# Decode rows laid out by head and token in the retention and state-space stages, and the last gate projection spread over the state-space tiles

## The chip, the cores and the metric

One core of a Trainium2 chip runs the whole program once per execution. The metric is device microseconds of that execution; the number compared is the median of several executions. Everything is float32.

## What is computed

A two-layer decoder trunk makes one inference step for two groups of rows with the same weights: a prompt of 512 tokens, and a sample group of 8 sequences with 4 tokens each (32 rows), which carries recurrent states from memory. Each layer projects the normalised input once (`w_in`), runs four mixers side by side, gates and merges their projections, projects back, and ends in a feed-forward block. Two mixers matter here. In both, every sample sequence `b` and head `h` has a 128x128 state that is read, used for the output, and written back:

```python
# retention, 4 heads; state-space (Mamba-2) has the same shape with B, C, x in place of k, q, v
intra = einsum('bhnm,bmhe->bnhe', scores, v)
cross = einsum('bnhd,bhde->bnhe', q * q_decay, S)
S_new = exp(log_gamma * C) * S + einsum('bmhd,bmhe->bhde', k * k_decay, v)
o = (o - mean(o)) * rsqrt(var(o) + eps) * silu(g)            # retention: per head
...
merged = sum_b sigmoid(gate_b) * (branch_b @ w_branch_b)     # gates: columns of h @ w_in
```

## The kernel before

All 544 rows (512 + 32) stay on chip. A layer is a chain of stages, each a block of five instruction streams (TensorE, VectorE, ScalarE, GpSimd, SyncE) written out by hand and tied by semaphores; all engines meet at a barrier between stages. The order is attention, retention (`stage_retention`), HGRN (`stage_hgrn`), state-space (`stage_ssm`: a convolution block, then the scan block), merge (`stage_merge`), feed-forward.

The mixers alone would leave TensorE idle, so the weight projections are dealt out among them. `jobs` lists the projections in order; the end of it is ..., gate20, wb11, gate21, wb20, gate30, wb21, gate31, wb30, wb31, wo0, wo1. A gate job is 64 matmuls (8 result rows of 8), a wb job 32 (8 rows of 4), each 128x128 by 128x272. The trace counts every float32 matmul as two records, so 16 records are 8 matmuls. A result row gets a PSUM bank from the set in `spare`; it must wait until the row that had the bank before has been taken out, by ScalarE for gates (with one sigmoid at the end of a job) and by VectorE for wb rows (a multiplication with the gate, L492, and an addition, L494). `Share(last, weights)` takes all matmuls up to the job `last` and cuts them at fixed points: where an engine's stream calls `share.point`, TensorE issues the matmuls up to that share, and ScalarE and VectorE take out rows that are done, one row behind. `stream` on SyncE loads the weights, each job into the slot of the job two before it, once that is finished.

Retention (L1285 to L1500) and the scan block of the state space (from L2087) run over five tiles: four of 128 prompt tokens, the fifth the 32 sample rows. The names used below:

- Retention, fifth tile. TensorE: scores L1327; fill; `A` times `v` L1335 and masked queries times states L1339 (8 per head, all writing rows 0 to 31 of bank 3), head by head, each waiting for a fresh mask `qm` from VectorE (L1431); then the added states `kd` times the spread values `Vx` L1355, eight matmuls that each wait for VectorE's update two before (L1442, a multiply-add; L1435 spreads `v` anew for every head); two points of fill; turning the result (L1361); fill. VectorE then normalises 32 rows of 512 (L1459 to L1469). SyncE stores the states (L1499).
- State space. Each tile: segment sums L2153; two points of fill; weights ready; outputs L2161, L2165, L2166 and the next tile's turns L2133 to L2137; two points of fill; wait for the finished rows `d_y`; turn them L2204; one point of fill. The fifth tile also turns the eight states and multiplies them (L2177, L2186), sums the decays (L2191, taken by ScalarE L2243), and updates the states: eight matmuls L2198, VectorE spreading `B` (L2305), decaying (L2308) and adding (L2309). The output chain on VectorE starts at L2318 and only after all updates. SyncE stores the sample states L2123, then the prompt state L2125.
- HGRN's fifth tile (L1638 on) has the layout that the change brings to the other two: rows by (head, token) on 128 partitions, so the four heads' matmuls use different strips of the array: L1683 for states, L1695 for updates, GpSimd decaying the states (L1563), VectorE adding (L1930), SyncE loading strips (L1953).
- `stage_merge` begins with gate31, then wb30.

Of the kernel before, what the change touches and what calls it, by code (L numbers as in the profile page):

```python
# [13 lines left out]
P = 128  # L14
# [28 lines left out]
for _n, _w in (("ident", 128), ("ones", 128), ("after", 128), ("tri", 128), ("lv_sum", 7 * 128), ("tri_s", 32), ("after_s", 32),  # L43
               ("seqhot", 8), ("qmask", 256), ("lv_mask", 6 * 32), ("lns", 1), ("rdec", 4 * 128), ("rq", 4), ("rk", 4), ("rdec_s", 4 * 32), ("rq_s", 4),
               ("rk_s", 4), ("cos", 5 * 64), ("sin", 5 * 64), ("neg", 128), ("neg_s", 32), ("eps", 1),
               ("rep", 2 * 128), ("wsel", 2 * NS), ("hsel", 8), ("sum4", NS), ("block", 1)):
    C[_n] = (_at, _w)
    _at += _w
# [4 lines left out]
def constants():  # L53
# [67 lines left out]
    put("block", r[:, None] % 32)  # L121
    put("hsel", (r[:, None] // TS) % 8 == np.arange(8)[None])
# [10 lines left out]
def trunk(nc, inp, out):  # L133

    es = ExitStack()
    with es:
# [187 lines left out]
        for name in ("gate30", "wb21"):  # L324
            spare[name] = (2, 6, 7)
        for name in ("gate31", "wb30", "wb31", "wo0", "wo1"):
# [961 lines left out]
        def stage_retention(l):  # L1288
# [10 lines left out]
            qm = ar.take(NB, NS)  # L1299
# [4 lines left out]
            Vx = sc.take(NB, P)  # L1304
            share = Share("wb01", [6] + [1] * 25)
            job0 = J["wb01"] - 1
            with nc.Block() as block:
                @block.tensor
                def _(pe):
# [10 lines left out]
                    for i, (t0, m) in enumerate(tiles):  # L1320
# [10 lines left out]
                        if last:  # L1331
                            pe.wait_ge(S("b_state_in"), 64)
                        for h in range(4):
                            o = ps[3][0:m, h * P:h * P + P]
                            mm = pe.matmul(o, A[0:m, h * m:h * m + m], v(i)[0:m, h * P:h * P + P], start=True, stop=(i == 0))  # L1335
                            if last:
                                pe.wait_ge(S("b_q_masked"), h + 1)
                                for b in range(NB):
                                    mm = pe.matmul(o, qm[:, b, :], S0[:, b, h, :], start=False, stop=(b == NB - 1))  # L1339
                                mm.then_inc(S("b_q_mask_used"), 1)  # L1340
                            elif i > 0:
                                mm = pe.matmul(o, qT[:, h * m:h * m + m], Sp[:, h, :], start=False, stop=True)
                        if not last:
                            for h in range(4):
# [3 lines left out]
                        else:  # L1348
                            for h in range(4):
                                pe.wait_ge(S("b_v_masked"), h + 1)  # L1350
                                for half in range(2):
                                    n = 2 * h + half
                                    if n >= 2:
                                        pe.wait_ge(S("b_state_new"), n - 1)
                                    pe.matmul(ps[n % 2][:, :], kd[i % 2][0:NS, h * P:h * P + P],  # L1355
                                              Vx[0:NS, half * 4:half * 4 + 4, :].rearrange("p b e -> p (b e)")).then_inc(S("b_state_add"), 1)
# [3 lines left out]
                        for h in range(4):  # L1360
                            mm = pe.transpose(ps[2][:, h * m:h * m + m], t2[0:m, h * P:h * P + P], ident[0:m, 0:m])  # L1361
                        mm.then_inc(S("b_y_turned"), 1)
                        share.point("pe", pe)
# [3 lines left out]
                def _(act):  # L1367
# [9 lines left out]
                    for i, (t0, m) in enumerate(tiles):  # L1377
# [6 lines left out]
                        ach.link(act, act.activation(sm[0:m, 1, :], sm[0:m, 1, :], ACT.Ln, bias=eps[0:m], scale=1.0 / P))  # L1384
                        act.activation(sm[0:m, 1, :], sm[0:m, 1, :], ACT.Exp, scale=-0.5).then_inc(S("b_rstd"), 1)
# [7 lines left out]
                def _(dve):  # L1393
# [25 lines left out]
                    for i, (t0, m) in enumerate(tiles):  # L1419
# [5 lines left out]
                        if last:  # L1425
                            dve.wait_ge(S("b_turn_taken"), i + 1)
                            msk = K("qmask").rearrange("p (b t) -> p b t", b=NB)
                            for h in range(4):
                                if h >= 1:
                                    dve.wait_ge(S("b_q_mask_used"), h)  # L1430
                                dve.tensor_tensor(qm, bc(qT[:, h * NS:h * NS + NS], 1, NB), msk, ALU.mult).then_inc(S("b_q_masked"), 1)  # L1431
                            for h in range(4):
                                if h >= 1:
                                    dve.wait_ge(S("b_state_add"), 2 * h)
                                dve.tensor_tensor(Vx[0:NS], bc(v(4)[0:NS, h * P:h * P + P], 1, NB), bc(K("seqhot")[0:NS], 2, P), ALU.mult).then_inc(S("b_v_masked"), 1)  # L1435
                                for half in range(2):
                                    n = 2 * h + half
                                    dve.wait_ge(S("b_state_add"), n + 1)
                                    if h == 0 and half == 0:
                                        dve.wait_ge(S("b_q_mask_used"), 4)  # L1440
                                    st = S0[:, half * 4:half * 4 + 4, h, :]
                                    dve.scalar_tensor_tensor(st, st, GAMMA[h] ** TS, ps[n % 2][:, :].rearrange("p (b e) -> p b e", b=4),  # L1442
# [1210 lines left out]
```

## Time and profile before

| | us |
|---|---|
| runs (3): lowest, median, highest | 3918.91, 3921.76, 3924.99 |
| the profiled execution | 3920.59 |
| its span, first to last instruction | 3918.7 |
| TensorE busy in the span | 3511.9 |
| VectorE, ScalarE, GpSimd busy | 1735.5, 727.9, 244.7 |
| mean granted clock of TensorE | 0.931 |

A granted clock of 1 is 2.4 GHz, 0.5 is 1.2 GHz. In a timeline a line reads: start, duration, engine, line of the code, operation, output <- input, shape, how many, and in brackets the engine's idle time before it and what ended that. PE is TensorE (PEld its weight loads), DVE VectorE, ACT ScalarE, POOL GpSimd, SPq SyncE's queue. L382 is the fill.

### The profile page before, as it was taken

What the parts mean: (1) busy time and instruction counts of PE and PEld (TensorE: products, weight loads), DVE (VectorE), ACT (ScalarE), POOL (GpSimd) and SP (SyncE); (2) the same over time, 40 slices, a digit from 0 to 9 for tenths busy, and PEclk for the clock granted to TensorE, in tenths of its full rate; (3) what the DMA queues carried; (4) which work ended last, traced back from release to release, by engine and by line L of the source; (5) the groups of instructions that cost most, each with busy time, mean ns of one, the idle gap of its engine ahead of it and who ended that gap; (6) DMA issues with size and microseconds to landing.
All of it is one profiled execution on the core that took longest, in us unless ns stands there. A gap on an engine that the chain in (4) does not pass through costs nothing. (4 is left out here: it accounts for less than half of the span.)

```text
span 3918.7 us, 45141 instructions
## 1 busy us (share of the span) xinstructions
PE 3511.9 (90%) x18090; PEld 2454.4 (63%) x18090; DVE 1735.5 (44%) x3249; ACT 727.9 (19%) x1550; POOL 244.7 (6%) x250
## 2 busy tenths in 40 slices
PE   5988899998988788999989889998988886989998
PEld 2643455576666566888846345555766674868887
DVE  2146295134545523454512653940445364144543
ACT  1222222111322200000012222221213221010000
POOL 0000321200100000000000004112000000000000
PEclk9989899888998889999999899997989997999999
DMA  3211355522314031222222114436231321212221
GB/s 118 86 60 39 109 180 169 179 88 91 108 39 131 25 100 44 86 86 70 70 93 92 39 49 153 159 134 223 83 111 55 96 66 57 87 47 82 86 78 64
DMA packets 274202, 365.83 MB, mean 93 GB/s; under 512 B 39006, under 2 KB 170462, under 8 KB 273860
## 3 DMA queue, kind: packets, MB, share of 16 engines
q1 hardware_dynamic: 231580, 260.59, 20.4%
q0 software_dynamic: 21504, 75.51, 6.0%
q10 hardware_dynamic: 20904, 26.78, 1.9%
q8 instruction: 146, 2.39, 0.3%
q14 instruction: 68, 0.56, 0.0%
HBM read 312.50 MB, written 50.34 MB: 93 GB/s over the span
## 5 line engine op out<-in xcount | busy, mean ns | idle before, releaser
L382 PE MATMUL ps<-hT,ring 128*128 128x272 f32 x3072 | 784.7, 411 | 81.4 <-PEq L154 54.8
L382 PEld LDWEIGHTS ps<-hT,ring 128*128 128x128 f32 x3072 | 596.8, 199 | 232.4 <-issue 77.0
L374 PE MATMUL ps<-ring,hT 128*128 128x512 f32 (+3 forms) x1600 | 656.8, 552 | 35.1 <-DVE hT L637 19.0
L374 PEld LDWEIGHTS ps<-ring,hT 128*128 128x128 f32 (+1 forms) x1600 | 279.7, 199 | 325.9 <-issue 301.6
L382 PE MATMUL ps<-branchT,ring 128*128 128x272 f32 x1024 | 271.5, 421 | 31.7 <-DVE arena L492 22.8
L2468 PE MATMUL ps<-hT,ring 128*128 128x272 f32 x1136 | 278.7, 396 | 17.4 <-DVE hT L637 17.4
L382 PEld LDWEIGHTS ps<-branchT,ring 128*128 128x128 f32 x1024 | 203.9, 204 | 93.2 <-DVE arena L492 27.6
L2468 PEld LDWEIGHTS ps<-hT,ring 128*128 128x128 f32 x1136 | 217.7, 192 | 63.5 <-issue 18.2
L961 DVE MAX8 branchT<-arena 32x8 f32<-32x2080 f32 x64 | 148.2, 2316 | 2.2
L962 DVE MATCH_REPLACE8 arena<-branchT,arena 32x2080 f32<-32x2080 f32 x64 | 147.0, 2297 | 0.0
L2468 PE MATMUL ps<-arena,ring 128*128 128x272 f32 x528 | 126.4, 393 | 2.8 <-DMA ring<-in_w_down 2.8
L382 PE MATMUL ps<-arena,ring 128*128 128x272 f32 x512 | 117.8, 393 | 2.2 <-issue 2.2
L2468 PEld LDWEIGHTS ps<-arena,ring 128*128 128x128 f32 x528 | 100.2, 190 | 24.2 <-DMA ring<-in_w_down 3.6
L382 PEld LDWEIGHTS ps<-arena,ring 128*128 128x128 f32 x512 | 97.1, 190 | 22.9 <-issue 3.0
L2468 PE MATMUL ps<-branchT,ring 128*128 128x272 f32 x448 | 111.2, 392 | 0.0
L2468 PE MATMUL ps<-branchT,arena 128*128 128x272 f32 x448 | 111.2, 392 | 0.0
L1200 ACT ACTIVATE branchT<-ps 128x512 f32<-128x512 f32 x128 | 69.5, 594 | 194.7 <-PE ps L1105 194.4
L2481 ACT ACTIVATE arena<-ps 128x272 f32<-128x272 f32 x60 | 23.8, 397 | 392.9 <-PE ps L2468 392.9
L2468 PEld LDWEIGHTS ps<-branchT,arena 128*128 128x128 f32 x448 | 85.1, 190 | 17.6
L2468 PEld LDWEIGHTS ps<-branchT,ring 128*128 128x128 f32 x448 | 85.1, 190 | 17.5
L733 DVE TENSOR_TENSOR branchT<-arena 128x2560 f32<-128x2560 f32 (+1 forms) x4 | 8.6, 2154 | 190.1 <-PEq L693 190.1
L2468 PE MATMUL ps<-branchT,stage 128*128 128x272 f32 x352 | 87.8, 392 | 0.0
(465 smaller groups left out, 4455.5 us busy)
## 6 DMA issues: line engine op xcount, KB each, us to landing
ring<-in_w_in SPq DMA_DIRECT2D x44, 2048.0 KB, 8.1
ring<-in_w_gu SPq DMA_DIRECT2D x44, 1024.0 KB, 6.5
spill<-stage ACTq DMA_DIRECT2D x72, 256.0 KB
arena<-spill SPq DMA_DIRECT2D x16, 1024.0 KB, 5.6
ring<-in_w_branch SPq DMA_DIRECT2D x16, 1024.0 KB, 5.3
ring<-in_w_down SPq DMA_DIRECT2D x8, 1536.0 KB, 6.6
ring<-in_w_down SPq DMA_DIRECT2D x8, 1280.0 KB, 5.8
ring<-in_w_out SPq DMA_DIRECT2D x4, 2048.0 KB, 9.8
```

Of the source, the lines that this page charges most:

```text
L374: mm = pe.matmul(bank[0:m, 0:w], hT[:, c, t0:t0 + m], slot3(j)[:, c, 0:w], start=(c == 0), stop=(c == kn - 1))
L382: mm = pe.matmul(bank[:, 0:HALF], slot3(j)[:, c, at:at + P], src, start=(c == 0), stop=(c == kn - 1))
L733: vch.link(dve, dve.tensor_tensor(t2, a2, a2, ALU.mult))
L961: vch.link(dve, dve.max(m, src))
L962: vch.link(dve, dve.match_replace(work, m, src, TAKEN))
L1200: act.activation(KT[:, bb, j, :], ps[j][:, :], ACT.Copy).then_inc(S("kt_ready"), 1)
L2468: mm = pe.matmul(bank(n, p), left[:, c, :], r[:, c, :], start=(c == 0), stop=(c == k - 1))
L2481: act.activation(part_of[n % 2][0], bank(n, 1), ACT.Copy).then_inc(S("p1_copied"), 1)
```

## The change

1. Retention, fifth tile: queries masked once for all heads into one `qm`; output rows laid on partitions (head, token), 32 columns of the array per head; `v` and `g` loaded again in that layout by eight strip DMAs; keys turned once and scaled by a new constant `rk_ht`; `v` spread once over 128 partitions; the normalisation on 128x128 in place of 32x512; the state updates moved behind the turned result, in two halves of four matmuls on four 32-row strips and four banks, with the last point of fill between the halves.
2. State space, fifth tile: `x`, `B` and the weights turned to the same layout by 12 small matmuls; GpSimd decays the states; the updates moved behind the turned result in two halves, as above; VectorE only adds.
3. The scan block's `Share` ends at gate31 in place of wb21 (160 matmuls in place of 96 over the same points); gate31 gets banks 2, 6, 7 in place of all eight; SyncE's loads move on by one job.

```diff
-        for name in ("gate30", "wb21"):
+        for name in ("gate30", "wb21", "gate31"):
             spare[name] = (2, 6, 7)
-        for name in ("gate31", "wb30", "wb31", "wo0", "wo1"):
+        for name in ("wb30", "wb31", "wo0", "wo1"):
             spare[name] = range(8)
...
# retention, TensorE, fifth tile
+                            pe.wait_ge(S("b_prompt_state"), 1)
+                            pe.transpose(ps[4][:, 0:P], kT[:, 0:P], ident).then_inc(S("b_k_turned"), 1)
+                            pe.wait_ge(S("b_state_in"), 64)
+                            pe.wait_ge(S("b_q_masked"), 1)
                             for h in range(4):
-                                pe.wait_ge(S("b_v_masked"), h + 1)
...
+                                pe.matmul(ps[3][h * NS:h * NS + NS, 0:P], A[0:NS, h * NS:h * NS + NS], v(4)[0:NS, h * P:h * P + P], start=True, stop=False)
+                            for b in range(NB):
+                                for h in range(4):
+                                    mm = pe.matmul(ps[3][h * NS:h * NS + NS, 0:P], qm[:, b, h * NS:h * NS + NS], S0[:, b, h, :], start=False, stop=(b == NB - 1))
+                            mm.then_inc(S("b_rows_out"), 1)
                         share.point("pe", pe)
                         share.point("pe", pe)
                         pe.wait_ge(S("b_y"), i + 1)
...
+                            pe.transpose(ps[2][:, 0:P], t2[:, 0:P], ident).then_inc(S("b_y_turned"), 1)
+                            pe.wait_ge(S("b_v_spread"), 1)
+                            pe.wait_ge(S("b_kd"), 1)
+                            for half in range(2):
+                                for h in range(4):
+                                    if half:
+                                        pe.wait_ge(S("b_state_new"), h + 1)
+                                    r = slice(h * NS, h * NS + NS)
+                                    pe.matmul(ps[added[h]][:, :], kds[r], Vx[r, half * 4:half * 4 + 4, :].rearrange("p b e -> p (b e)")).then_inc(S("b_state_add"), 1)
+                                if half == 0:
+                                    share.point("pe", pe)
...
# state space
-            share = Share("wb21", [1, 4] + [2, 2, 2, 2, 1] * 5)
-            job0 = J["wb21"] - 1
+            share = Share("gate31", [1, 4] + [2, 2, 2, 2, 1] * 5)
+            job0 = J["gate31"] - 1
...
+                @block.gpsimd
+                def _(pool):
+                    pool.wait_ge(S("ssm_in"), 64)
+                    pool.wait_ge(S("ssm_decays"), 1)
+                    pool.wait_ge(S("hs_turned"), 8)
+                    for half in range(2):
+                        for q in range(4):
+                            st = h0[:, half * 4:half * 4 + 4, q, :]
+                            pool.tensor_tensor(st, st, bc(dec[:, q, half * 4:half * 4 + 4], 2, P), ALU.mult).then_inc(S("ssm_decayed"), 1)
...
+                            for q in range(4):
+                                r = slice(q * NS, q * NS + NS)
+                                pe.matmul(ps[0][r, 0:P], xc[:, q, SEQ:T], ident)
+                                pe.matmul(ps[0][r, P:2 * P], xc[:, 4 + q // 2, SEQ:T], ident)
+                                mm = pe.matmul(ps[0][r, 2 * P:2 * P + 2], ident[0:NS, 0:NS], wt[0:NS, 2 * q:2 * q + 2])
+                            mm.then_inc(S("d_rows"), 1)
...
# state space, VectorE, fifth tile: ahead of the output chain
+                            dve.wait_ge(S("ssm_decays"), 1)
                             dve.wait_ge(S("hs_used"), 8)
...
+                            dve.tensor_tensor(Bx, bc(qt[:, P:2 * P], 1, NB), bc(K("hsel"), 2, P), ALU.mult).then_inc(S("b_spread"), 1)
...
# and behind d_y_turned
+                            for half in range(2):
+                                for q in range(4):
+                                    n = 4 * half + q
+                                    dve.wait_ge(S("ssm_add"), n + 1)
+                                    dve.wait_ge(S("ssm_decayed"), n + 1)
+                                    st = h0[:, half * 4:half * 4 + 4, q, :]
+                                    dve.tensor_tensor(st, st, ps[added[q]][:, :].rearrange("p (b s) -> p b s", b=4), ALU.add).then_inc(S("ssm_new"), 1)
+                                if half == 0:
+                                    share.point("dve", dve)
```

The four matmuls of half 0 write banks 0, 1, 4 and 3 (`added`). Retention's VectorE does the same as the last piece with its multiply-add, after the normalisation.

## Rows read from the trace of the kernel before

**Rows 1.** The page, busy time of each engine.

```profile
PE 3511.9 (90%) x18090; PEld 2454.4 (63%) x18090; DVE 1735.5 (44%) x3249; ACT 727.9 (19%) x1550; POOL 244.7 (6%) x250
```

**Rows 2.** Busy by stretch (us): PE, PEld, DVE, ACT, POOL, clock, DMA; last two: layer 1.

```profile
943.50:970.60 27.10, 20.84 (x89) 10.83 (x88) 10.58 (x14) 2.01 (x2) 0.00 (x0) 0.77 0.16 59
...
1384.50:1397.40 12.90, 0.00 (x0) 0.03 (x1) 0.88 (x2) 0.00 (x0) 0.00 (x0) 0.50 0.90 265
1397.40:1429.10 31.70, 31.70 (x128) 25.95 (x129) 0.00 (x0) 2.79 (x7) 0.00 (x0) 0.93 0.00 1
...
2872.20:2899.40 27.20, 20.94 (x89) 10.82 (x88) 10.58 (x14) 1.95 (x2) 0.00 (x0) 0.77 0.15 58
...
3313.00:3326.00 13.00, 0.03 (x1) 0.00 (x1) 0.88 (x2) 0.00 (x0) 0.00 (x0) 0.50 0.83 262
```

**Rows 3.** Timeline of retention's fifth tile, layer 0.

```profile
943.87 1.94 PE L1339 MATMUL ps<-arena 128*32 128x128 f32 x16
...
970.65 10.42 PE L382 MATMUL ps<-branchT,ring 128*128 128x272 f32 x34
...
985.95 0.45 SPq L1499 DMA_DIRECT2D out_ret_sample<-arena  x1
...
988.38 6.05 PE L382 MATMUL ps<-hT,ring 128*128 128x272 f32 x18 [3.09 <-PEq L154]
```

**Rows 4.** Timeline of HGRN's fifth tile, layer 0, where the new layout runs.

```profile
1107.78 5.53 SPq L1953 DMA_DIRECT2D arena<-spill  x12
...
1151.38 1.96 PE L1683 MATMUL ps<-arena,branchT 128*32 128x128 f32 x64
...
1153.54 8.02 POOL L1563 TENSOR_TENSOR arena<-arena,branchT 128x512 f32<-128x512 f32 x8 [37.22 <-PE ps L1683]
...
1155.75 1.14 PE L1695 MATMUL ps<-branchT,stage 32*128 32x512 f32 x8
1156.91 4.45 DVE L1930 TENSOR_TENSOR arena<-arena,ps 128x512 f32<-128x512 f32 x7 [2.05 <-PE ps L1695]
```

**Rows 5.** Timeline of the state space's tiles 0, 1 and 3, layer 0.

```profile
1256.67 2.00 PE L2161 MATMUL ps<-arena 128*128 128x64 f32 x16
...
1266.44 0.66 PE L2204 MATMUL ps<-cst,arena 128*128 128x128 f32 x4 [2.09 <-DVE arena L2332]
...
1269.64 3.83 PE L382 MATMUL ps<-hT,ring 128*128 128x272 f32 x16
...
1273.31 1.89 PE L2161 MATMUL ps<-arena 128*128 128x64 f32 x16
...
1286.02 1.10 PE L2204 MATMUL ps<-cst,arena 128*128 128x128 f32 x4 [4.72 <-DVE arena L2332]
...
1327.05 0.42 DVE L492 TENSOR_TENSOR arena<-ps,xT 128x272 f32<-128x272 f32 x1
...
1327.53 1.27 PE L382 MATMUL ps<-branchT,ring 128*128 128x272 f32 x2 [2.95 <-DVE arena L492]
```

**Rows 6.** Timeline of the state space's fifth tile, layer 0.

```profile
1334.78 0.69 PE L2153 MATMUL ps<-cst,arena 32*32 32x32 f32 x16 [0.69 <-ACT arena L2258]
...
1352.95 1.05 PE L2191 MATMUL ps<-cst,arena 32*128 32x8 f32 x8
...
1354.27 1.21 DVE L2305 TENSOR_TENSOR arena<-arena,cst 32x1024 f32<-32x1024 f32 x1 [13.21 <-ACT arena L2243]
...
1373.53 0.68 DVE L2318 TENSOR_TENSOR arena<-arena,layer_params 32x512 f32<-32x512 f32 x1
...
1381.74 0.63 PE L2204 MATMUL ps<-cst,arena 32*128 32x32 f32 x4 [1.67 <-DVE arena L2332]
...
1385.80 8.13 SPq L2125 DMA_DIRECT2D out_ssm_prompt<-arena  x1
```

**Rows 7.** Timeline of HGRN's first instructions, GpSimd beside VectorE.

```profile
988.76 1.26 POOL L1552 TENSOR_TENSOR arena<-arena,layer_params 128x512 f32<-128x512 f32 x1
989.07 1.50 DVE L1802 TENSOR_TENSOR arena<-arena,layer_params 128x512 f32<-128x512 f32 x1
```

More of the change, by code:

```diff
@@ L1330, in _ @@
                         pe.wait_ge(S("b_weights"), i + 1)
[L1331 to L1342, printed above, removed]
[L1343 removed]
+                        if not last:
+                            for h in range(4):
+                                o = ps[3][:, h * P:h * P + P]
+                                mm = pe.matmul(o, A[:, h * m:h * m + m], v(i)[:, h * P:h * P + P], start=True, stop=(i == 0))
+                                if i > 0:
+                                    mm = pe.matmul(o, qT[:, h * m:h * m + m], Sp[:, h, :], start=False, stop=True)
                             for h in range(4):
@@ L1470, in _ @@
                         share.point("dve", dve)
-                        share.point("dve", dve)
+                        if last:
+                            for half in range(2):
+                                for h in range(4):
+                                    dve.wait_ge(S("b_state_add"), 4 * half + h + 1)
+                                    st = S0[:, half * 4:half * 4 + 4, h, :]
+                                    dve.scalar_tensor_tensor(st, st, GAMMA[h] ** TS, ps[added[h]][:, :].rearrange("p (b e) -> p b e", b=4),
+                                                             ALU.mult, ALU.add).then_inc(S("b_state_new"), 1)
+                                if half == 0:
+                                    share.point("dve", dve)
+                        else:
+                            share.point("dve", dve)
@@ L2333, in _ @@
                         dve.wait_ge(S("d_y_turned"), i + 1)
-                        share.point("dve", dve)
+                        if last:
+                            for half in range(2):
+                                for q in range(4):
+                                    n = 4 * half + q
[3 more added lines that the diff above has]
+                                    dve.tensor_tensor(st, st, ps[added[q]][:, :].rearrange("p (b s) -> p b s", b=4), ALU.add).then_inc(S("ssm_new"), 1)
+                                if half == 0:
+                                    share.point("dve", dve)
+                        else:
+                            share.point("dve", dve)
                     share.end("dve", dve)
```

112 lines of the change are left out of this document (55 added, 57 removed).

## The prediction

> **What bounds the kernel now.** The busy times come first: TensorE works for nine tenths of the span, the others for less than half [rows 1]. So an edit pays only where it shortens TensorE's work or fills its pauses. The busy times by stretch then show where its pauses and slow stretches are. In retention's fifth tile 27.1 us hold 89 records, a granted clock of 0.77, and 6.3 us of nothing; behind the state space TensorE stands for 12.9 us, and gate31 then takes 31.7 us by itself. Layer 1 repeats both stretches to 0.1 us [rows 2], so everything below is worked out for layer 0 and doubled. The timelines show what TensorE waits for inside these stretches [rows 3, 5, 6], and HGRN's fifth tile shows the new layout at work [rows 4].
>
> **Retention.** From 943.5, where the weights are ready, to 970.6 [rows 2] TensorE does the outputs and state updates, each behind a VectorE operation. In the new order:
> - Outputs. Masked queries times states took 1.94 us per head of 16 records, four times; HGRN does all 64 in 1.96 us, since its heads use different columns of the array [rows 3, 4]. One mask operation of 1.2 us (as long as the 1024 columns of [rows 6]) ends before TensorE is through the fill ahead. With a turn and the `A` products (0.5 us, my estimate from the same rows' rate) the outputs end at 946.0.
> - Two points of fill, 17 matmuls. Eight take 3.67 us from start to start [rows 5], so 0.459 each and 7.8 us: to 953.8. Before, they took 10.4 us [rows 3], part of it at the lower clock. VectorE's output chain is seven operations; even at 0.7 us each, the price of 32x512 [rows 6], they end by 951.5 with ScalarE's part, so the chain is covered by fill. Without the fill it would cost 5 us.
> - Turn and half 0, 0.2 and 1.14 us as in HGRN [rows 4]: 955.2. Fill of 8 matmuls: 3.7 us, plus 0.9 us for one bank, since wb01's row is taken out only behind the four multiply-adds of half 0 (2.8 us): 959.8.
> - Half 1 has no fill left behind it. Its first multiply-add starts 0.7 us on, four of 0.69 us follow, two rows are taken out: VectorE ends at 964.2, SyncE has issued its store by then, and TensorE restarts 2.0 us later (from 986.4, the end of the store's issue, to 988.38 [rows 3]): 966.2.
> - Eight strip DMAs sit on SyncE between the state loads and the third tile's load. Twelve took 5.5 us [rows 4], so 3.7 us; the third tile's load waits some 30 us for a buffer anyway, so they cost nothing; without that wait it would be 3.7 us once.
>
> 988.4 against 966.2 is **22.2 us a layer**; the bounds are 20 (VectorE's chain and half 1 at the lower clock) and 24.5 (no wait for the bank).
>
> **State space, tiles 0 to 3.** The points now hold 160/96 of the matmuls: a pair of points 12.8 in place of 7.7 (5.9 us in place of 3.5), the single one 3.2 (1.5 in place of 0.9), the opening 16 in place of 10.
> - Before the outputs L2161, TensorE had to wait only as long as its pair of points lasts (tile 1: 1269.64 to 1273.31 [rows 5]); the longer pair is paid there, 2.2 us a tile.
> - Between outputs and turned rows, the output chain on VectorE decides: 1273.31 to 1286.02 is 12.7 us, of which TensorE stood 4.7 [rows 5]. The longer pair fits in, and 2.4 us of the pause go. In tile 0 it is 9.8 us, 2.1 of them idle [rows 5], and it just fits too.
> - Taking out wb21's rows (a multiplication of 0.42 us [rows 5] and an addition as long, 0.94 with gaps) moves from tiles 3 and 4 to tile 2: three of them, 2.8 us, lie inside its chain; tile 3's chain is 1.3 us shorter for it, and its weights come without the lower clock.
>
> The start of the fifth tile's sums (1334.8 [rows 6]) so moves by +5.8 (opening and tile 0), +1.9, +5.5, -1.8: **+11.4 us**, with 52.5 matmuls (24.1 us) more done by then.
>
> **State space, fifth tile.** The pair before the outputs adds 2.5 us, the 12 turning matmuls 0.7 us (24 records at the rate of L1683 [rows 4]; one after the other, as L1339 runs [rows 3], 2.9). The loop over eight states keeps its 14 us, to L2191's end, before at 1354.0 [rows 6]: shift 14.6 us.
> - From there to the turned rows it took 27.7 us (to 1381.74 [rows 6]): updates, then chain. Now the updates are out of the way: `B` spread once (1.2 us), seven operations of 0.7, ScalarE's 0.8, two more operations of 0.7: 8.6 us if VectorE is alone. The fill (5.9 us) is over before that.
> - But GpSimd decays eight pieces in just this time, 8.0 us alone [rows 4]. Where GpSimd and VectorE both worked from the on-chip memory, VectorE's product took 1.50 us beside GpSimd's 1.26 [rows 7], where 32x512 alone takes 0.68 [rows 6]; HGRN's additions, which read PSUM, kept 4.45/7 = 0.64 us beside GpSimd [rows 4]. Of VectorE's operations here the spread and six others read only the on-chip memory; the six carry 1.50 - 0.68 = 0.8 us more each, 4.9 us, and the spread, which starts first, an estimated 0.7. The bounds are nothing (GpSimd slips into VectorE's gaps) and 7; I take 5.6, the row nearest in kind. So 14.2 us, shift now 1.1.
>
> The Trainium skill (SBUF — State Buffer, "SBUF: two separate sides") has this as an exclusive lock held for the whole instruction, the loser blocking fully. By that rule each of the six would wait out one decay of 1.0 us [rows 4], 6.2 us in place of 4.9; the trace agrees in kind, and the time by the rule would be 2.6 us more, 3831.
>
> - Tail. From the turned rows to TensorE's restart it was 15.7 us: to 1385.80 the last fill, then 8.13 us in which SyncE issues the prompt state's store, then the barrier [rows 2, 6]. Now half 0, the last fill at the lower clock (2.9 us, since TensorE has stood for 8 us), and half 1 with four additions lie ahead of the stores: 9.2 us to the last addition in place of some 3.4. That is +5.9: shift 7.0. ScalarE's sigmoid of gate31 ends at about the same time as the additions and is covered by the stores.
> - gate31's 31.7 us [rows 2] then drop out of the merge stage. The cold start after the pause goes over to wb30.
>
> 31.7 - 7.0 = **24.7 us a layer**; with the bounds of the two open prices 21 to 31.
>
> **Sum.** 2 x (22.2 + 24.7) = 93.8. The profiled execution took 3920.6 us for a span of 3918.7; its 3920.6 becomes 3826.8. The median of the runs is 1.2 us above that execution, so **3828 us**. This forecast's own range is 3805 to 3845.
>
> **Rivals.**
> - *The chain runs free.* GpSimd's decays cost VectorE nothing, and tiles 1 and 3 stay at full clock. For it: HGRN's additions beside the same decays [rows 4]. Against it: [rows 7]. It gives 5.6 a layer more: 3817 us.
> - *The fill is not hidden.* gate31's 64 matmuls lengthen every tile by their full 29.4 us, because the pauses shift to other points of the tile. For it: three of five points in a tile show no pause at all [rows 5]. Against it: the 4.7 us in front of the turned rows. Then only the fifth tile gains, 13.5 less 5.9 of tail, 7.7 a layer: 3921.8 - 2 x (22.2 + 7.7) = 3862 us.
> - *Strips one after the other.* The four strips don't overlap: retention's outputs take 4 x 1.94 us, 5.8 more [rows 3]; the state space's turns 2.2 more; each half four times 0.86 us (512 columns at the fill's rate) in place of 1.14, 2.3 more, four halves. That is 17 us a layer: 3862. HGRN's rows speak against it [rows 4]. It is also the case in which the layout doesn't do what it is for.
> - *Slower: three banks.* gate31's rows must each wait until ScalarE has taken out the row three before, which it does a point late, behind its part of each tile. TensorE then stands at each of gate31's last five rows. One such wait is in the trace, 2.95 us on VectorE at a wb21 row [rows 5]; five of these on top of the unhidden fill give 3862 + 30 = 3892. It turns into a loss from 6 us a row, 2 x 30 = 60 in all; with 8 us it is 3942. Against it: gates are taken out in 0.4 us, and no wait in any tile is on ScalarE.
>
> **How the numbers follow.** Forecast 0.57; free chain 0.20; fill not hidden 0.13; strips 0.05; three banks beyond the turning point 0.03; the pieces cancelling to nothing 0.02. The predicted time is the forecast's. The range runs from 3804 (free chain and the upper bounds) to 3860, which leaves out about half of the unhidden fill and of the strips, the null case and the slower one. A measurement of this kernel tells about 0.2% from no change, 8 us; all but the last two cases are beyond that, so faster 0.95, same 0.02, slower 0.03.
>
> **What would show it.** Right: the four heads' output matmuls of retention as one row of 64 records near 2 us; retention's pause before HGRN grown from 3 to some 6 us; no gate31 in the merge stage; the pause before each L2204 about halved; VectorE's 32x512 products at 1.4 us and more beside GpSimd in the fifth tile. Wrong: a pause of TensorE at gate31 rows with ScalarE as releaser; fifth-tile products at 0.68 us (free chain); a tail before the merge stage well over 16 us.

## The result, and the profile after

The kernel before was run again beside the changed one:

| | before | after |
|---|---|---|
| median of the runs (us) | 3923.38 | 3827.71 |
| lowest, highest | 3918.91, 3929.58 | 3825.75, 3829.94 |
| the profiled execution | 3920.59 | 3829.94 |
| its span | 3918.7 | 3827.8 |

The ratio is 0.9755 (95% interval 0.9738 to 0.9772): 95.7 us less, where 3828 was forecast. The busy times of the page answer to [rows 1]:

```profile
PE 3452.2 (90%) x18134; PEld 2424.6 (63%) x18134; DVE 1713.0 (45%) x3223; ACT 727.3 (19%) x1552; POOL 264.0 (7%) x266
```

TensorE has 44 records more and 59.7 us less of busy time, of a span 90.9 us shorter: two thirds of the gain is work that runs faster, strips side by side and less of it at 1.2 GHz, and the rest is pauses filled. In layer 0, TensorE's busy time from the scores of retention's fifth tile to HGRN falls from 39.72 to 21.02 us, and the granted clock there rises from 0.83 to 0.94; in the state space's fifth tile, from its sums to the restart behind it, the clock rises from 0.74 to 0.85.

**Retention.** The timeline of TensorE over the fifth tile in layer 0, and SyncE's last line in it, answer to [rows 3]. L1332 is the scores, L1352 and L1355 the outputs, L383 the fill, L1373 the first of the two halves of the updates:

```profile
940.78 0.44 PE L1332 MATMUL ps<-branchT 128*32 128x32 f32 x8
...
945.47 1.96 PE L1355 MATMUL ps<-arena,branchT 128*32 128x128 f32 x64
947.36 8.06 PE L383 MATMUL ps<-branchT,ring 128*128 128x272 f32 x34
...
955.46 1.14 PE L1373 MATMUL ps<-branchT 32*128 32x512 f32 x8
...
959.50 2.10 PE L383 MATMUL ps<-branchT,ring 128*128 128x272 f32 x8 [0.87 <-DVE arena L490]
...
965.20 0.40 SPq L1520 DMA_DIRECT2D out_ret_sample<-arena  x1
...
967.90 6.22 PE L383 MATMUL ps<-hT,ring 128*128 128x272 f32 x18 [5.23 <-PEq L155]
```

The scores of the kernel before, for comparison:

```profile
939.31 0.44 PE L1327 MATMUL ps<-branchT 128*32 128x32 f32 x8
```

All 64 records of queries times states take 1.96 us, as long as one head's 16 did [rows 3]. The wait of 0.87 us for the bank and the pause of 5.2 us before HGRN stand where the prediction put them. From the scores to HGRN's first fill it is 27.12 us; before it was 49.07 (scores at 939.31, fill at 988.38 [rows 3]): **21.95 us less**.

**State space, tiles 1 to 3.** The waits that TensorE has left between the first outputs and the sums of the fifth tile, from the timeline of layer 0 (L2238 turns the finished rows):

```profile
1269.43 1.18 PE L383 MATMUL ps<-branchT,ring 128*128 128x272 f32 x4 [1.74 <-ACT arena L421]
...
1294.25 4.00 PE L383 MATMUL ps<-branchT,ring 128*128 128x272 f32 x8 [4.27 <-DVE arena L493]
...
1321.96 0.66 PE L2238 MATMUL ps<-cst,arena 128*128 128x128 f32 x4 [1.61 <-DVE arena L2372]
```

Before, TensorE stood in front of the turned rows of tiles 0 to 3 for 2.09, 4.72, 4.27 and 1.61 us, and for 2.95 us at a wb21 row in tile 3 ([rows 5] has three of these). Now nothing is left of that in tiles 0 and 2, 0.43 us in tile 1, and in tile 3 the same 1.61 without the 2.95. What is left in tile 2 stands at a row of wb21 that needs a bank: with three banks TensorE waits 4.27 us for VectorE to take an older row out, behind its output chain. The waits with ScalarE as releaser are at wb21's rows and short; gate31's rows (`hT`) never wait.

**State space, fifth tile.** TensorE, answering to [rows 6]: L2208 to L2210 are the turning matmuls of one strip, L2232 the decay sums, and the two last lines wb30 with wb31, and wo0:

```profile
1332.90 0.41 PE L2208 MATMUL ps<-cst,arena 128*32 128x128 f32 x2
1333.14 0.38 PE L2209 MATMUL ps<-cst,arena 128*32 128x128 f32 x2
1333.45 0.22 PE L2210 MATMUL ps<-arena,cst 32*32 32x2 f32 x2
...
1335.71 1.09 PE L2218 MATMUL ps<-cst,branchT 128*128 128x128 f32 x8
...
1348.30 1.05 PE L2232 MATMUL ps<-cst,arena 32*128 32x8 f32 x8
...
1361.59 0.52 PE L2238 MATMUL ps<-cst,arena 32*128 32x32 f32 x3 [6.08 <-DVE arena L2372]
...
1380.52 31.62 PE L383 MATMUL ps<-branchT,ring 128*128 128x272 f32 x128 [12.10 <-PEq L155]
1413.26 7.11 PE L383 MATMUL ps<-arena,ring 128*128 128x272 f32 x30 [1.11 <-issue]
```

The other engines in the same stretch: VectorE's output chain beside GpSimd's eight decays, then SyncE's stores:

```profile
1349.62 1.23 DVE L2350 TENSOR_TENSOR arena<-arena,cst 128x1024 f32<-128x1024 f32 x1 [13.04 <-ACT arena L2291]
1350.76 1.52 DVE L2358 TENSOR_TENSOR arena<-arena,layer_params 32x512 f32<-32x512 f32 x1
1352.32 0.67 DVE L2359 TENSOR_TENSOR arena<-arena,ps 32x512 f32<-32x512 f32 x1
...
1354.77 1.42 DVE L2363 TENSOR_TENSOR arena<-arena 32x512 f32<-32x512 f32 x1
...
1357.67 0.68 DVE L2365 TENSOR_REDUCE arena<-arena 32x2 f32<-32x512 f32 x1
...
1349.73 11.26 POOL L2144 TENSOR_TENSOR branchT<-branchT,arena 128x512 f32<-128x512 f32 x8 [192.26 <-ACT arena L2291]
...
1371.55 5.29 SPq L2160 DMA_DIRECT2D out_ssm_prompt<-arena  x1
```

The eight decays take 11.26 us in place of 8.02 alone [rows 4], and VectorE's operations with two operands in the on-chip memory up to 1.52 in place of 0.68.

The scan block's first matmul and the first of wo0 before the change, and the first matmul after it:

```profile
1243.16 1.09 PE L2133 MATMUL ps<-cst,arena 128*128 128x128 f32 x4 [3.49 <-PEq L1981]
...
1459.75 6.43 PE L382 MATMUL ps<-arena,ring 128*128 128x272 f32 x27 [1.11 <-issue]
```

```profile
1221.51 1.09 PE L2168 MATMUL ps<-cst,arena 128*128 128x128 f32 x4 [3.50 <-PEq L2002]
```

Counted from that first matmul (1243.16 before, 1221.51 after), the shifts in layer 0 are:

| point | forecast | measured |
|---|---|---|
| start of the fifth tile's sums (1334.78; 1325.12) | +11.4 | +12.0 |
| end of the decay sums (1354.00; 1349.35) | +14.6 | +17.0 |
| turned rows (1381.74; 1361.59) | +1.1 | +1.5 |
| TensorE's restart (1397.40; 1380.52) | +7.0 | +4.8 |
| wb30's start (1429.14; 1380.52) | -24.7 | -27.0 |
| wo0's start (1459.75; 1413.26) | not given | -24.8 |

Layer 1 shows the stages of layer 0: scores to HGRN's first fill 27.12 us, decay sums to turned rows 12.24, turned rows to restart 18.53.

### The profile page after: what moved, and what is told of

Its sections match the earlier page's. It is cut to its first block and busy times, and to the rows that moved or that the text cites. A ratio compares the mean times of both kernels' runs of the same rounds, so it can differ in the third digit from the quotient of the medians.

```text
span 3827.8 us, 45249 instructions
## 1 busy us (share of the span) xinstructions
PE 3452.2 (90%) x18134; PEld 2424.6 (63%) x18134; DVE 1713.0 (45%) x3223; ACT 727.3 (19%) x1552; POOL 264.0 (7%) x266
## 5 line engine op out<-in xcount | busy, mean ns | idle before, releaser
L383 PE MATMUL ps<-hT,ring 128*128 128x272 f32 x3072 | 779.4, 409 | 61.8 <-PEq L155 32.3
L383 PEld LDWEIGHTS ps<-hT,ring 128*128 128x128 f32 x3072 | 592.3, 198 | 213.4 <-issue 56.5
L383 PE MATMUL ps<-branchT,ring 128*128 128x272 f32 x1024 | 269.9, 419 | 63.0 <-PEq L155 24.2
L383 PEld LDWEIGHTS ps<-branchT,ring 128*128 128x128 f32 x1024 | 201.7, 202 | 123.3 <-issue 32.5
L383 PE MATMUL ps<-arena,ring 128*128 128x272 f32 x512 | 117.8, 393 | 2.2 <-issue 2.2
L383 PEld LDWEIGHTS ps<-arena,ring 128*128 128x128 f32 x512 | 97.1, 190 | 22.9 <-issue 3.0
L2519 PEld LDWEIGHTS ps<-branchT,arena 128*128 128x128 f32 x448 | 85.1, 190 | 17.6
```

The costliest lines, as they stand in the source:

```text
L383: mm = pe.matmul(bank[:, 0:HALF], slot3(j)[:, c, at:at + P], src, start=(c == 0), stop=(c == kn - 1))
L2519: mm = pe.matmul(bank(n, p), left[:, c, :], r[:, c, :], start=(c == 0), stop=(c == k - 1))
```

## The experiments

My theory, after the two traces: the two halves of the change add up; retention's gain is the strips working side by side; the state space gains by the spread gate projection and by its new layout, and gives part of that back in three places: turning matmuls one behind the other, VectorE and GpSimd in each other's way, one slow store in the tail. The rivals stand with each run. Stages are read beside whole times, since whole times of one program wander, as the repeat at the end shows.

**Retention alone.** The hunks of retention and its constants; the state space keeps

```diff
-            share = Share("gate31", [1, 4] + [2, 2, 2, 2, 1] * 5)
+            share = Share("wb21", [1, 4] + [2, 2, 2, 2, 1] * 5)
...
```

and all else of before.

> The retention half of the change alone; the state-space tiles and the last gate projection stay as before. My theory is that the two halves simply add: the new layout of the sample tile takes 22 us out of each layer's retention stage (scores of the fifth tile to the projection that follows: 49.1 us before, 27.1 after), and nothing later in the layer takes it up. That gives 3923.4 - 44 = about 3879 us. The rival is that the halves interact (loads that come due earlier, the state space starting at another clock): then the retention stage shows the same 22 us and the whole something other than 44, below 35 or above 50.

Measured 3882.29 us (ratio 0.9891, 0.9875 to 0.9908), 39.5 us under the 3921.79 of before in the same runs. Scores to HGRN's first fill is 27.12 us in both layers. The state space, from the scan block's first matmul to wo0, takes 217.7 and 217.5 us in the two layers, where it was 216.6 in both before. So the halves add, but for 1 us a layer.

**The gate projection not spread.**

```diff
-            share = Share("gate31", [1, 4] + [2, 2, 2, 2, 1] * 5)
-            job0 = J["gate31"] - 1
+            share = Share("wb21", [1, 4] + [2, 2, 2, 2, 1] * 5)
+            job0 = J["wb21"] - 1
```

with gate31's eight banks of before.

> The change without dealing out the last gate projection: the fifth state-space tile keeps its new layout, the second block of the third branch is dealt out once more, and the gate projection goes back behind the merge. My theory is that the new layout alone takes 8 to 10 us per layer out of the state space, and that the dealt-out gate fills waits of the tiles worth some 17 us per layer: about 3828 + 34 = 3862 us, with the pauses of tile 3 in front of its y matmuls back near 4 us each. The rival, that the chain of the tiles would have run freely and the gate's matmuls only moved, says no loss: 3828, within 8.

Measured 3867.88 us (0.9855, 0.9825 to 0.9885). In its timeline, the scan block's first matmul, two waits of TensorE (tiles 2 and 4), and the first matmuls of wo0:

```profile
1226.06 1.09 PE L2168 MATMUL ps<-cst,arena 128*128 128x128 f32 x4 [3.49 <-PEq L2002]
...
1290.52 1.12 PE L2238 MATMUL ps<-cst,arena 128*128 128x128 f32 x4 [4.26 <-DVE arena L2372]
...
1349.49 2.18 PE L383 MATMUL ps<-branchT,ring 128*128 128x272 f32 x4 [6.45 <-DVE arena L493]
...
1433.35 6.88 PE L383 MATMUL ps<-arena,ring 128*128 128x272 f32 x29 [1.11 <-issue]
```

The pauses are back: 4.26 us in front of tile 2's turned rows, and 6.45 us in the fifth tile for a bank with a wb21 row; tile 3 has 2.95 and 2.16, not the 4 expected. By whole times the spreading would be worth 40 us and the new layout of the fifth tile 14, but the executions of this run lie 20 us apart (3853.34 to 3873.84). The stage is firmer: from the scan block's first matmul to wo0 it is 207.3 and 207.4 us here, 217.7 and 217.5 with retention alone, and 191.7 and 191.9 in the changed kernel. So the new form of the fifth tile is worth some 10 us a layer and the spreading of gate31 15.6, close to the 8 to 10 and 17 that were expected; what of the 10 us is the layout, and what the move of the updates behind the turned rows, was not tried. About half of gate31's 29.4 us is hidden, the other half lengthens the tiles, and the rival of the unhidden fill falls.

**Heads one after the other in retention.**

```diff
-                                pe.matmul(ps[3][h * NS:h * NS + NS, 0:P], A[0:NS, ...
+                                o = ps[3][0:NS, h * P:h * P + P]
+                                pe.matmul(o, A[0:NS, ...
+                                for b in range(NB):
+                                    mm = pe.matmul(o, qm[:, b, h * NS:h * NS + NS], S0[:, b, h, :], ...
```

The turn and the normalisation of the fifth tile go back to 32 rows of 512 with it.

> Retention's output matmuls write all four heads on the same 32 rows again (heads side by side in the columns), with the masks still made once and the updates still behind the outputs; norm and turning go back to 32 rows of 512. My theory is that the four row strips work at the same time in the changed kernel and one after the other here: the 36 output matmuls go from 2.4 us to about 8 us, the norm of the chain behind grows by less than 1 us and stays under the fill, so about 5.5 to 6 us more per layer, 3839 us. The rival is that only the removal of the mask waits between the heads counted, and the strips share nothing: then the 36 matmuls take the same 2.4 us and the time stays at 3828, within 4.

Measured 3845.18 us (0.9804, 0.9788 to 0.9821). The last head, the fill behind it, and HGRN's first fill, on TensorE:

```profile
951.04 1.94 PE L1355 MATMUL ps<-arena,branchT 128*32 128x128 f32 x16
952.90 2.56 PE L383 MATMUL ps<-branchT,ring 128*128 128x272 f32 x10
956.42 5.77 PE L383 MATMUL ps<-branchT,ring 128*128 128x272 f32 x24 [0.96 <-DVE arena L490]
...
974.81 6.57 PE L383 MATMUL ps<-hT,ring 128*128 128x272 f32 x18 [5.23 <-PEq L155]
```

With no mask to wait for, each head still takes 1.94 us: it was the strips. The time from the scores (939.78) to the first fill behind the outputs grows by 6.54 us, and the longer chain on VectorE (0.68 in place of 0.29 us per operation) adds a wait of 0.96 us for a bank, which the expectation had put under the fill. From the scores to HGRN's first fill it is 35.03 us in both layers, against 27.12 in the changed kernel. So the mechanism is the theory's, and 7.9 us a layer in place of its 5.5 to 6; the rival falls.

**Retention's updates where they stood,** run twice.

```diff
+                            for half in range(2):
+                                for h in range(4):
+                                    ...
                         share.point("pe", pe)
                         share.point("pe", pe)
                         pe.wait_ge(S("b_y"), i + 1)
```

> The sample rows stay by head and token, but retention's state updates stand straight behind the outputs again, as they did before the change, and the fill is not put between the two halves. My theory is that the layout gives retention's gain and the move behind the turning hides little: the eight update matmuls and their eight VectorE additions would stand ahead of the norm, and the fill that covers the norm is still there. I expect the stage (scores to restart) within 1.5 us of the changed kernel's 27.1, so 3828 within 4. The rival is that the move is what hides the updates: then the norm starts some 6 us later, the turning and the tail behind it too, and 4 to 6 us per layer come back, 3836 to 3840.

Measured 3837.95 us (0.9782, 0.9766 to 0.9798). And again:

> Retention's updates in place, once more: its first timing stood at 3838, 10 us over the changed kernel, while its profiled execution (3831) has both layers' retention within 3 us of the changed kernel, one above and one below. If the move is worth those 10 us (the rival's 4 to 6 us per layer), the time repeats at 3836 to 3840 and the stage in a profile is longer by that in both layers. If they came from where the low-clock stretches fell, the time comes back to within 4 us of the changed kernel beside it, or the stage again shows no such loss.

Measured 3833.66 us (0.9778, 0.9759 to 0.9797), with the changed kernel at 3826.84 beside it. One of the updates' waits in the kernel before; then the updates, the fill behind them and HGRN's first fill in layer 0 of the second run (scores at 940.10):

```profile
956.97 2.40 PE L1355 MATMUL ps<-branchT 32*128 32x512 f32 x4 [1.90 <-DVE branchT L1435]
```

```profile
946.67 1.14 PE L1364 MATMUL ps<-branchT 32*128 32x512 f32 x8
948.64 2.91 PE L1364 MATMUL ps<-branchT 32*128 32x512 f32 x8 [0.83 <-DVE arena L1451]
951.49 2.56 PE L383 MATMUL ps<-branchT,ring 128*128 128x272 f32 x10
...
967.33 4.36 PE L383 MATMUL ps<-hT,ring 128*128 128x272 f32 x18 [3.25 <-PEq L155]
```

From the scores to HGRN's first fill, the two layers of the first run take 29.82 and 27.24 us, those of the second 27.24 and 29.82. In all nine profiled executions that have retention as changed it is 27.11 or 27.12 in every layer. So the updates in place cost 0.1 us where the granted clock of the stretch is 1.00, and 2.7 where it is 0.89; the expected 1.5 us holds for one layer of two, and a stage that is 4 to 6 us longer was not seen. The whole is 7 to 10 us slower all the same, which the expectation gave to the rival; 2.8 of that is in the stage, and where the rest comes from is open.

The updates themselves are the largest piece of retention's gain. Before, it was 17.6 us from the first of them (953.09) to the fill behind them (970.65 [rows 3]), at a granted clock of 0.65 and with three waits of 1.90 us for `v` to be spread anew; here, at a clock of 1.00, it is 4.8 (946.67 to 951.49). No run separates the four strips of the updates from the single spread of `v` and the four banks, so of retention's 21.95 us a layer only the 7.9 that the run with one strip gave back is shown to be the strips.

**GpSimd's decays behind the output chain.**

```diff
                     pool.wait_ge(S("hs_turned"), 8)
+                    pool.wait_ge(S("d_y"), 5)
```

> GpSimd's eight state decays of the fifth state-space tile wait until VectorE has finished that tile's y. My theory is that the two engines slow each other there: VectorE's operations on the sample rows, 1.4 to 1.5 us each in the changed kernel, fall back to about 0.68, the pause ahead of the turning of y falls from 6.1 us to about 2.3, and the decays still end before the state additions need them. That takes 3.8 us from each layer: about 3820 us. The rival is that the decays then are late: at 1.0 to 1.4 us each, eight of them from about the end of y on, the additions of the second half wait for them, and the tail behind grows by as much or more: 3828 to 3836. A second rival is that the operations are slow for their own shape and operands: then they stay near 1.4 us and nothing is won.

Measured 3825.78 us (0.9757, 0.9743 to 0.9770). One of VectorE's operations, GpSimd's decays, and the turned rows on TensorE:

```profile
1359.26 0.68 DVE L2364 TENSOR_TENSOR arena<-arena 32x512 f32<-32x512 f32 x1
...
1363.53 8.04 POOL L2145 TENSOR_TENSOR branchT<-branchT,arena 128x512 f32<-128x512 f32 x8 [201.13 <-DVE arena L2373]
...
1363.41 0.37 PE L2239 MATMUL ps<-cst,arena 32*128 32x32 f32 x3 [2.24 <-DVE arena L2373]
```

Both engines are back at their times alone, the pause is 2.24 in place of 6.08, and decay sums to turned rows is 8.40 us in place of 12.24: 3.84 us in each layer. Six of the state additions now wait for a decay, 0.31 us each, as the first rival had it, but the tail behind the turned rows has not grown: 18.55 and 18.52 us, against 18.93 and 18.53. The stage is as the theory had it and both rivals fall. The whole shows 2 of the 7.7 us: in the profiled execution TensorE was at tile 0's sums at 1237.80, 9.3 us later than in the changed kernel run again below, in code that is the same up to there.

**The prompt's store ahead of the stream.**

```diff
+                    sp.wait_ge(S("ssm_prompt_ready"), 1)
+                    sp.dma_start(out["ssm_prompt"][lay]...
                     ...
-                    sp.wait_ge(S("ssm_prompt_ready"), 1)
-                    sp.dma_start(out["ssm_prompt"][lay]...
```

> The store of the prompt's state is issued on SyncE's queue ahead of the stream of the next projection's loads and not behind it. My theory is that the tail of the state space (y turned to restart, 18.9 us) ends on that one issue, 5.3 us on a queue that has to wait for it; issued early it leaves the tail, and ScalarE's last sigmoid of the gate projection, which ends 8 us before the restart, is the next bound: 4 to 5 us less per layer, about 3818 us. The rival is that the issue is slow wherever it stands, because the descriptors of the loads fill the rings: then the loads are late by the same time and the restart stays where it is: 3828, within 4.

Measured 3825.81 us (0.9757, 0.9743 to 0.9770). SyncE's two stores, ScalarE's table load behind gate31's sigmoid, and TensorE's restart:

```profile
1326.41 0.40 SPq L2157 DMA_DIRECT2D out_ssm_prompt<-arena  x1
...
1371.76 0.40 SPq L2160 DMA_DIRECT2D out_ssm_sample<-branchT  x1
...
1372.01 1.28 ACT L426 ACT_TABLE_LOAD   x1
...
1376.82 8.54 PE L383 MATMUL ps<-branchT,ring 128*128 128x272 f32 x26 [7.58 <-PEq L155]
```

The issue takes 0.40 us where the one ahead of it on the queue began 26 us earlier, and 5.29 straight behind the sample states' store. Turned rows to restart is 14.05 and 14.18 us, 4.9 and 4.4 less; ScalarE, done at 1373.3, is the new end. The rival falls by the stage, not by the whole, which again shows 2 of 9 us.

**The turning matmuls by kind.**

```diff
                             for q in range(4):
-                                pe.matmul(ps[0][r, 0:P], xc[:, q, SEQ:T], ident)
-                                pe.matmul(ps[0][r, P:2 * P], xc[:, 4 + q // 2, SEQ:T], ident)
-                                mm = pe.matmul(ps[0][r, 2 * P:2 * P + 2], ...
+                                pe.matmul(ps[0][rows[q], 0:P], xc[:, q, SEQ:T], ident)
+                            for q in range(4):
+                                pe.matmul(ps[0][rows[q], P:2 * P], xc[:, 4 + q // 2, SEQ:T], ident)
+                            for q in range(4):
+                                mm = pe.matmul(ps[0][rows[q], 2 * P:2 * P + 2], ...
```

> The twelve turning matmuls of the fifth state-space tile are issued by kind (four of x, four of B, four of the weights) and not row strip by row strip. My theory is that they took 2.8 us because the three of one strip stand one behind the other, and that neighbours on different strips overlap: about 0.8 us, 2.0 us less per layer, 3824 us. The rival is that the time goes into loading their stationary operands or into their 12 starts, in any order: then 2.8 us and 3828.

Measured 3816.80 us (0.9735, 0.9722 to 0.9748; five runs within 1.1 us).

```profile
1330.20 0.43 PE L2208 MATMUL ps<-cst,arena 128*32 128x128 f32 x8
1330.44 0.40 PE L2210 MATMUL ps<-cst,arena 128*32 128x128 f32 x8
1330.77 0.24 PE L2212 MATMUL ps<-arena,cst 32*32 32x2 f32 x8
1330.94 1.16 PE L2220 MATMUL ps<-cst,branchT 128*128 128x128 f32 x8
```

The same 24 records, four strips in turn, take 0.74 us in place of 2.81. The stage is 2.07 us shorter in each layer, as expected, and the rival falls. The order by kind changes a second thing: among the twelve, the shape of the array's part that a matmul takes (128*32 or 32*32 in the lines) changes once in place of seven times. Where the shape stays, from x to B, one strip takes 0.24 us from start to start, and four strips by kind take the same 0.24, so there it is the strips; what the changes of shape cost by themselves was not tried. The whole is 10 us shorter, of which this accounts for 4.

**The three together, and two of them.** All three edits as above, then without

```diff
-                    pool.wait_ge(S("d_y"), 5)
```

> The three edits together: decays behind y, the prompt's store ahead of the stream, the turning matmuls by kind. If each takes out its own piece of one chain (3.8, 4.5 and 2.0 us per layer) the sum is 10.3 per layer: about 3807 us. The rival is that they stand on parallel branches and the slowest one decides: then the gain is that of the largest, 3818, or, if the late decays set the tail, nothing.

> The prompt's store ahead of the stream and the turning matmuls by kind, without the late decays. By the stages of the single edits (4.9 and 2.1 us per layer) the two are 14 us under the changed kernel, 3814; with the late decays they measured 3812.7. If the late decays add their 3.8 us per layer to the whole, this run stands 7 us above that one, near 3820; if what they win ahead of the turning of y is lost behind it (the state additions then wait for GpSimd one by one), it stands within 3 us of it.

Three: 3812.71 us (0.9724, 0.9710 to 0.9737). Two: 3823.67 us (0.9738, 0.9721 to 0.9755). TensorE in the tail of the three:

```profile
1360.96 0.37 PE L2241 MATMUL ps<-cst,arena 32*128 32x32 f32 x3 [2.24 <-DVE arena L2375]
...
1374.03 6.25 PE L383 MATMUL ps<-branchT,ring 128*128 128x272 f32 x14 [6.91 <-PEq L155]
```

From the fifth tile's sums to the restart it is 43.6 us in both layers with three edits, 48.3 and 47.8 with two, 55.4 and 55.0 in the changed kernel. So what the late decays win ahead of the turned rows is not paid back behind them. The two whole times are 11 us apart where their stages differ by 8.8 in both layers together, and they stand 4 to 6 us above the 3807 and 3820 of the expectations. With three, 11.4 to 11.8 us a layer are gone from the stage; the ratio to before (0.9724, up to 0.9737) lies below that of the changed kernel run again (0.9759, from 0.9742), some 14 us: this version is faster than both kernels.

**The changed kernel again.**

> The changed kernel once more, unaltered, beside the two kernels below, so that differences of a few us between them can be read at all. 3828 us, within 5. The local stages (scores to restart of retention 27.1 us, turned y to restart of the state space 18.9 us) should repeat to 0.1 us, while the place of the low-clock stretches need not.

Measured 3826.84 us (0.9759, 0.9742 to 0.9777), scores to HGRN's first fill 27.11 us, turned rows to restart 18.95 and 18.93. Its span was 3821.6, 6.2 us under the first execution's. The busy times by stretch (PE, PEld, DVE, ACT, POOL, clock, DMA) for one stretch of HGRN, first in the first execution:

```profile
1040.00:1060.00 20.00, 17.91 (x164) 11.85 (x163) 12.57 (x33) 4.76 (x10) 2.54 (x2) 0.83 0.15 54
```

and in the second:

```profile
1040.00:1060.00 20.00, 16.65 (x277) 11.32 (x275) 14.92 (x37) 4.74 (x8) 3.98 (x2) 1.00 0.15 54
```

The granted clock in this window is 0.83 and 1.00. The windows do not hold the same records, since the second execution gets further in the same time; one group of matmuls that lies in both, first in the first execution, is

```profile
1041.48 4.67 PE L1607 MATMUL ps<-cst,arena 128*128 128x512 f32 x8
```

```profile
1040.01 3.77 PE L1607 MATMUL ps<-cst,arena 128*128 128x512 f32 x8
```

At tile 0's sums in the state space, the two executions of one program are 2.8 us apart in layer 0 and 8.0 in layer 1. A whole time therefore doesn't price an edit of 2 to 5 us a layer; the stages do, equal to 0.1 us from run to run in most cases and to 0.8 where such a stretch falls into one (tiles 0 to 3: 103.6 and 104.4 us). The run of the turns by kind reached tile 0's sums in layer 0 as early as this repeat (1228.6 and 1228.5) and in layer 1 earlier (3105.9 and 3109.2), which its own edit, 2 us a layer, explains in part.

## Why the prediction was right, step by step

The stages of layer 0 give 2 x (21.95 + 24.8) = 93.5 us, against 93.8 forecast and 95.7 by the medians.

**Retention** was right: 22.2 forecast, 21.95 measured, with the bank wait, the covered chain and the store's tail in their places. The eight strip DMAs cost nothing that can be seen.

**The four heads side by side** held for the outputs (1.96 us) and the halves (1.14 us), and the run with one strip shows that it is the strips. For the twelve turning matmuls it did not hold: the step "the 12 turning matmuls 0.7 us" took the wrong one of its own two ends, and 2.81 us was measured against its other end of 2.9. The text had not looked at the order of issue, three of one strip together. The run by kind gets 0.74 from the same matmuls.

The Trainium skill (TensorEngine Tiling (Array Packing), "Key Properties") says that different tiles can load weights and multiply in parallel. The two orders agree with that where neighbours in the order of issue are on different strips: x and B of one strip, one behind the other, are 0.24 us apart, and the x of all four strips take no longer than that.

**VectorE beside GpSimd** was right in kind and too large: 5.6 us forecast, 3.84 taken away by the late decays. Of that term the six two-operand operations cost 0.84, 0.31, 0.74, 0.74, 0.46 and 0.73, 3.8 together in place of 4.9, and the spread nothing (1.23 against 1.21 [rows 6]) in place of 0.7; it began 0.11 us ahead of the first decay. The operations with one operand in PSUM (0.67) and the reduction (0.68) kept their time. With the late decays the whole stretch is 8.40 us, against the 8.6 that the forecast had for VectorE alone (the terms it lists make 8.3).

The Trainium skill (SBUF — State Buffer, "Who interferes with whom") says so: a VectorE instruction with two inputs in the on-chip memory contends with a GpSimd instruction that reads it, and one with at most one such input, outside the two-port modes, does not. The trace agrees for the operations between the spread and the turn: the six with two such inputs are the ones that are hit. By its full block each would wait for up to a whole decay; the measured waits are shorter, the largest 0.84 us beside decays of 1.41.

**The tail** was too long: 21.6 us forecast, 18.93 measured. The term that failed is the prompt store's issue, taken over at 8.13 us [rows 6]; it was 5.29. That the tail ends on it was right, as the early store shows. The forecast's sign of failure, a tail well over 16 us, contradicted its own 21.6.

**gate31's 31.7 us** was the one bookkeeping fault. The text said that the cold start goes over to wb30, and still subtracted all of it: wb30 and wb31 take 31.62 us after the pause in place of 29.50. So the layer gains 24.8 at wo0, not the 27.0 at wb30. Two terms too pessimistic (contention 1.8, tail 2.7) and two too optimistic (turns 2.1, cold start 2.1) cancelled, and 24.7 came out right with four terms of the wrong size: the mechanisms held but for the turning matmuls, and that the number met to 0.1 us is luck.

**Tiles 0 to 3** were right in sum, 11.4 against 12.0; term by term the forecast had +5.8, +1.9, +5.5 and -1.8, and the starts of the tiles' sums give +4.4, +2.6, +7.5 and -2.5. In the third, the pause in front of the turned rows was replaced by 4.27 us for a bank, on VectorE and not, as the slower rival had it, on ScalarE at gate31's rows. The sign given for this, each pause in front of the turned rows about halved, did not hold tile by tile: two are gone, one is almost gone, and the last is as it was.

**Rivals.** The free chain falls by the 3.84 us, the unhidden fill by the run without the spread gate (were nothing of the fill hidden, taking it back would have cost next to nothing; it cost 15.6 us a layer), the strips by the run with one strip, apart from the turns; three banks held TensorE up, but before gate31 and for less than 6 us a row.

## What to carry to other kernels

Matmuls that are to share the array by strips are best issued as neighbours, a different strip each time; three of one strip in a row took 2.81 us here, near the 2.9 estimated for no sharing at all, and 0.74 in the other order. Work that moves to an idle engine may do better to start when the engine on the path is through with the memory that both read, if what waits for it can bear that; here that won 3.84 us a layer. When a projection was taken from behind a pause, the slow start stayed with the pause (31.62 us for the two projections that now come first, in place of 29.50). Edits of a few us are priced by the stage that they touch, not by the whole.

## What was not expected of the hardware

The issue of one store of the same data cost 0.40 us on SyncE's queue ahead of the stream, and 5.29 behind the sample states' store, where before the change it cost 8.13 [rows 6]; why these two differ was not tried. The issue ahead of the sample states' store, a load of weights, began 0.5 us before that store in the kernel before and 3.7 us before it in the changed one. And one program's executions, the same instruction for instruction, came 2.8 and 8.0 us apart to the same points, and in the stretch shown above the difference is the granted clock.
